# Dealing expert units to three weight streams, and taking a norm's root before its reciprocal

## What is computed

```python
def rmsnorm(x, g):                       # four times in the first block
    return x * rsqrt(mean(x * x) + 1e-6) * g

def layer_norm(x, g, b):                 # four times in the second block
    xc = x - mean(x)
    return xc * rsqrt(mean(xc * xc) + 1e-6) * g + b

def hier_moe(h, ...):                    # once in each of two layers
    # each token takes one of 4 groups and in it the best 2 of 8 experts
    ...
    order = jnp.argsort(flat_e)
    counts = jnp.bincount(flat_e, length=32)
    # the tokens of each expert are padded to whole blocks
    def run(args):
        xb, e = args
        return (jax.nn.silu(xb @ w1[e]) * (xb @ w3[e])) @ w2[e]
    ...
    # each token gets the sum of its two experts' rows, weighted by the gates
```

## Time and profile before

| | us |
|---|---|
| runs (three) | 3443.96, 3446.84, 3448.02; median 3446.84 |
| the profiled execution's own time | 3443.93 |
| its span, first to last instruction | 3442.1 |
| PE busy | 2927.2 (85% of the span) |
| DVE busy | 1152.2 (33%) |
| ACT busy | 681.0 (20%) |
| GpSimd busy | 123.5 (4%) |
| granted TensorE clock, mean | 0.920 of full |
| HBM read, written | 611.4 MB, 37.2 MB |

### The profile page before, as it was taken

The page is one execution under the profiler, slowest core; times in us unless marked ns, Lnnn a source line. Parts: engine busy times, 40 slices in busy tenths (PEclk is TensorE's granted clock), DMA queues, the critical chain, the costliest instruction groups (busy, mean ns, idle before and its releaser), DMA issues. The chain is left out here.

```text
span 3442.1 us, 38147 instructions
## 1 busy us (share of the span) xinstructions
PE 2927.2 (85%) x14080; PEld 1621.7 (47%) x14081; DVE 1152.2 (33%) x2252; ACT 681.0 (20%) x1368; POOL 123.5 (4%) x185
## 2 busy tenths in 40 slices
PE   6979867897999988996885989899688785999995
PEld 3435545544444443555553545444444543554553
DVE  2330178605887312026534111111323723111113
ACT  2430146401000000114422000000121521000002
POOL 0000000000000000000000100000100001000100
PEclk9999979998999998997996999999788897999997
DMA  4222200025755421110014999999712015999993
GB/s 171 81 77 86 108 7 1 0 73 144 299 220 204 174 79 61 61 49 31 0 54 166 389 407 394 403 405 411 273 60 80 0 54 199 396 394 416 375 409 124
DMA packets 137721, 631.50 MB, mean 183 GB/s; under 512 B 19270, under 2 KB 32966, under 8 KB 86560
## 3 DMA queue, kind: packets, MB, share of 16 engines
q1 hardware_dynamic: 93280, 418.20, 31.9%
q10 hardware_dynamic: 34992, 191.12, 13.8%
q0 software_dynamic: 9360, 21.00, 1.7%
HBM read 611.39 MB, written 37.22 MB: 188 GB/s over the span
## 5 line engine op out<-in xcount | busy, mean ns | idle before, releaser
L158 PE MATMUL psum<-normed,weight_ring 128*128 128x512 f32 x1472 | 642.9, 599 | 36.3 <-PEq L192 17.8
L158 PEld LDWEIGHTS psum<-normed,weight_ring 128*128 128x128 f32 x1472 | 282.8, 192 | 393.4 <-issue 393.4
L2106 PE MATMUL psum<-weight_ring,slot_rows_turned 128*64 128x256 f32 x3456 | 397.2, 383 | 1.0 <-issue 1.0
L2106 PEld LDWEIGHTS psum<-weight_ring,slot_rows_turned 128*64 128x64 f32 x3456 | 246.4, 138 | 147.2 <-issue 33.2
L2106 PE MATMUL psum<-third_stream_weights,slot_rows_turned 128*64 128x256 f32 x1728 | 219.6, 412 | 61.9 <-DMA third_stream_weights<-in_w_dram 61.8
L949 DVE SCALAR_TENSOR_TENSOR psum<-weight_ring,condition_rows 128x1024 f32<-128x1024 f32 x192 | 236.9, 1234 | 15.4 <-issue 0.9
L158 PE MATMUL psum<-modulated,weight_ring 128*128 128x384 f32 (+2 forms) x640 | 228.7, 518 | 0.0
L2238 DVE COPY expert_hidden_turned<-psum 128x256 f32<-128x256 f32 x81 | 34.3, 424 | 513.4 <-PE psum L2114 513.4
L2106 PEld LDWEIGHTS psum<-third_stream_weights,slot_rows_turned 128*64 128x64 f32 x1728 | 131.3, 149 | 149.9 <-DMA third_stream_weights<-in_w_dram 70.2
L2121 PE MATMUL psum<-weight_ring,expert_hidden_turned 128*64 128x512 f32 x864 | 197.2, 598 | 0.0
L2229 DVE COPY slot_rows_turned<-psum 128x512 f32<-128x512 f32 x81 | 56.0, 691 | 402.7 <-PE psum L2085 402.7
(11 more groups left out here) (362 smaller groups left out, 3069.4 us busy)
## 6 DMA issues: line engine op xcount, KB each, us to landing
weight_ring<-in_w_dram SPq DMA_DIRECT2D x114, 2048.0 KB, 15.1
third_stream_weights<-in_w_dram ACTq DMA_DIRECT2D x81, 2048.0 KB, 19.1
weight_ring<-in_w_ada_dram SPq DMA_DIRECT2D x24, 2048.0 KB, 9.9
weight_ring<-in_w_ffn_dram SPq DMA_DIRECT2D x11, 2048.0 KB, 7.8
expert_rows<-expert_rows ACTq DMA_DIRECT2D x162, 128.0 KB, 12.6
weight_ring<-in_w_rnn_dram SPq DMA_DIRECT2D x8, 1536.0 KB, 14.1
weight_ring<-in_w_att_dram SPq DMA_DIRECT2D x6, 2048.0 KB, 7.6
weight_ring<-in_w_in_dram SPq DMA_DIRECT2D x6, 2048.0 KB, 9.6
```

The costliest lines, as they stand in the source:

```text
L158: last = nc.tensor.matmul(out, weights[:, k * P:(k + 1) * P], rhs(k), start=(k == 0), stop=(k == tiles - 1))
L2106: last = nc.tensor.matmul(ps[64 * o:64 * o + 64, 2 + b, 256 * m:256 * (m + 1)], XT[:, b, k % 4, 64 * (k // 4):64 * (k // 4) + 64], w[:, k, ...
```

## The change

1. `rms_norms` and `layer_norm`: ACT takes the root of the variance straight from PSUM, with epsilon as the bias (a column `c.eps`, filled once), and DVE takes the reciprocal of the root just before it scales that piece. The additions are gone, and so is the signal from DVE to ACT; ACT waits for PE's variance instead. In `rms_norms` piece 0 is scaled before piece 1 is inverted.
2. `route`: experts other than 0 and 31 with one unit or none are `single`, the others `several`. With `nfirst = n - 2 * nhalf`, the `several` that end past `nfirst` are moved behind all singles, and the singles forward by as many units. Stream 0 takes only units 0 to nfirst-1 (so that it comes short where n is no multiple of three), the third stream the nhalf units from nfirst on, stream 1 the last nhalf as before. The table's third expert and the keys follow `nfirst` in place of `nhalf`.
3. The constants of the router have 32 more columns (`inner`), and the table's columns are 24 in place of 20.

The code of the experts' stage itself is not changed.

```diff
@@ -149,6 +149,7 @@
         c.nc.vector.memset(c.mean_w[:, :], 1.0 / D)
         if c.stat_count == 1:
             c.nc.vector.memset(c.ones[:, :], 1.0)
+            c.nc.vector.memset(c.eps[:, :], EPS)
 yield
 
 
...
@@ -201,8 +202,10 @@
                 finished.wait(act, (s - 1) * npiece + i + 1)
             nc.scalar.activation(sq[:, :, cols(i)], src[:, :, cols(i)], ACT.Square).then_inc(squared.sem, 1)
         for i in range(npiece):
-            inverted.wait(act, s * npiece + i + 1)
-            nc.scalar.activation(c.rstd[:, cols(i)], c.rstd_sq[:, cols(i)], ACT.Sqrt).then_inc(rooted.sem, 1)
+            u = s * npiece + i
+            var_ready.wait(act, u + 1)
+            nc.scalar.activation(c.stat[:, cols(i)], ps[:, u, 0:NORM_WIDTH], ACT.Sqrt, bias=c.eps[:, 0:1])\
+                .then_inc(rooted.sem, 1)
 
 @block.tensor
 def _(pe):
...
@@ -218,15 +221,11 @@
 v = nc.vector
 for s, (src, gain, out, add_to) in enumerate(stages):
     for i in range(npiece):
-        u = s * npiece + i
-        var_ready.wait(dve, u + 1)
-        v.tensor_scalar(c.stat[:, cols(i)], ps[:, u, 0:NORM_WIDTH], EPS, None, ALU.add)
+        rooted.wait(dve, s * npiece + i + 1)
+        v.reciprocal(c.rstd[:, cols(i)], c.stat[:, cols(i)])
+        if first and i == 0:
+            dve.wait_ge(c.consts_landed, 16 * len(c.const_loads))
         dve.drain()
-        v.reciprocal(c.rstd_sq[:, cols(i)], c.stat[:, cols(i)]).then_inc(inverted.sem, 1)
-    if first:
-        dve.wait_ge(c.consts_landed, 16 * len(c.const_loads))
-    for i in range(npiece):
-        rooted.wait(dve, s * npiece + i + 1)
         for k in range(KT):
             last = v.scalar_tensor_tensor(out=out[:, k, cols(i)], in0=src[:, k, cols(i)],
                                           scalar=c.vec(gain, k), in1=c.rstd[:, cols(i)],
...
@@ -1649,16 +1648,12 @@
 if 2 <= step < npiece + 2:
     i = step - 2
     rooted.wait(dve, i + 1)
+    v.reciprocal(VAR[:, 1, cols(i)], VAR[:, 0, cols(i)])
+    dve.drain()
     for k in range(KT):
         x = X[:, k, cols(i)]
-        v.scalar_tensor_tensor(out=x, in0=x, scalar=c.vec(gain, k), in1=ROOT[:, cols(i)],
+        v.scalar_tensor_tensor(out=x, in0=x, scalar=c.vec(gain, k), in1=VAR[:, 1, cols(i)],
                                op0=ALU.mult, op1=ALU.mult).then_inc(scaled.sem, 1)
-if 1 <= step < npiece + 1:
-    i = step - 1
-    var_ready.wait(dve, i + 1)
-    v.tensor_scalar(VAR[:, 0, cols(i)], ps[:, i, 0:WIDTH], EPS, None, ALU.add)
-    dve.drain()
-    v.reciprocal(VAR[:, 1, cols(i)], VAR[:, 0, cols(i)]).then_inc(inverted.sem, 1)
 if modulated and 3 <= step < npiece + 3:
     i = step - 3
     shifted.wait(dve, i + 1)
...
@@ -1683,8 +1678,9 @@
     a.activation(SQ[:, :, cols(step)], X[:, :, cols(step)], ACT.Square).then_inc(squared.sem, 1)
 if 1 <= step < npiece + 1:
     i = step - 1
-    inverted.wait(act, i + 1)
-    a.activation(ROOT[:, cols(i)], VAR[:, 1, cols(i)], ACT.Sqrt).then_inc(rooted.sem, 1)
+    var_ready.wait(act, i + 1)
+    a.activation(VAR[:, 0, cols(i)], ps[:, i, 0:WIDTH], ACT.Sqrt, bias=c.eps[:, 0:1])\
+        .then_inc(rooted.sem, 1)
 if 2 <= step < npiece + 2:
     i = step - 2
     for k in range(KT):
...
@@ -1896,17 +1892,40 @@
 v.tensor_reduce(nunits, units, AX, ALU.add)
 v.tensor_scalar(TS[:, 0, 0:NEXP], units, 1.0, None, ALU.min)
 dve.drain()
+second_from, third_by, turned_by, at = (TC[:, 13 + n:14 + n] for n in (0, 1, 2, 5))
+nfirst, nsingle, nmoved = (TC[:, 20 + n:21 + n] for n in range(3))
+single, several, scratch = TS[:, 3, 0:NEXP], TS[:, 3, NEXP:NKEY], TS[:, 4, 0:NEXP]
 v.tensor_tensor(earlier, by_pair(rank, 1), by_pair(rank, 2), ALU.is_gt)
-dve.drain()
-v.tensor_tensor(earlier, earlier, by_pair(units, 1), ALU.mult)
-dve.drain()
-v.tensor_reduce(base, earlier, AX, ALU.add)
-dve.drain()
-v.tensor_tensor(ends, base, units, ALU.add)
 v.scalar_tensor_tensor(out=TS[:, 1, 0:NEXP], in0=count[:, 1:NEXP + 1], scalar=float(NSTREAM),
                        in1=nunits.broadcast_to([P, NEXP]), op0=ALU.mult, op1=ALU.is_lt, accum_out=nrounds)
 v.tensor_scalar(TC[:, 10:11], nunits, 3.0, 1.0, ALU.mult, ALU.add)
 v.tensor_scalar(TC[:, 17:18], nunits, 3.0, -4.0, ALU.mult, ALU.add)
+v.scalar_tensor_tensor(out=single, in0=units, scalar=1.0, in1=const("inner"), op0=ALU.is_le, op1=ALU.mult)
+dve.drain()
+v.tensor_tensor(earlier, earlier, by_pair(units, 1), ALU.mult)
+v.tensor_scalar(nhalf, nrounds, 1.0, None, ALU.add)
+v.scalar_tensor_tensor(out=scratch, in0=single, scalar=1.0, in1=units, op0=ALU.mult, op1=ALU.mult,
+                       accum_out=nsingle)
+v.tensor_tensor(several, const("inner"), single, ALU.subtract)
+dve.drain()
+v.tensor_reduce(base, earlier, AX, ALU.add)
+v.scalar_tensor_tensor(out=nfirst, in0=nhalf, scalar=-2.0, in1=nunits, op0=ALU.mult, op1=ALU.add)
+v.tensor_tensor(second_from, nunits, nhalf, ALU.subtract)
+dve.drain()
+v.tensor_tensor(ends, base, units, ALU.add)
+v.tensor_scalar(third_by, nfirst, -3.0, 2.0, ALU.mult, ALU.add)
+v.scalar_tensor_tensor(out=turned_by, in0=nfirst, scalar=3.0, in1=TC[:, 17:18], op0=ALU.mult, op1=ALU.add)
+v.tensor_scalar(at, const("number"), nfirst, None, ALU.add)
+dve.drain()
+v.scalar_tensor_tensor(out=several, in0=ends, scalar=nfirst, in1=several, op0=ALU.is_gt, op1=ALU.mult)
+dve.drain()
+v.scalar_tensor_tensor(out=base, in0=several, scalar=nsingle, in1=base, op0=ALU.mult, op1=ALU.add)
+v.scalar_tensor_tensor(out=scratch, in0=several, scalar=-1.0, in1=units, op0=ALU.mult, op1=ALU.mult,
+                       accum_out=nmoved)
+dve.drain()
+v.scalar_tensor_tensor(out=base, in0=single, scalar=nmoved, in1=base, op0=ALU.mult, op1=ALU.add)
+dve.drain()
+v.tensor_tensor(ends, base, units, ALU.add)
 
 oh = OH[:, :, 0:nt, :]
 both = lambda n: V1[:, n, :, 0:nt]
...
@@ -1922,18 +1941,12 @@
 v.tensor_tensor(jb, n4(both(8), NCAPS - 1), row4(caps[:, 1:], NCAPS - 1), ALU.is_ge)
 dve.drain()
 v.tensor_reduce(b, jb, AX, ALU.add)
-v.tensor_scalar(nhalf, nrounds, 1.0, None, ALU.add)
-dve.drain()
-second_from, third_by, turned_by, at = (TC[:, 13 + n:14 + n] for n in (0, 1, 2, 5))
-v.tensor_tensor(second_from, nunits, nhalf, ALU.subtract)
-v.tensor_scalar(third_by, nhalf, -3.0, 2.0, ALU.mult, ALU.add)
-v.scalar_tensor_tensor(out=turned_by, in0=nhalf, scalar=3.0, in1=TC[:, 17:18], op0=ALU.mult, op1=ALU.add)
-v.tensor_scalar(at, const("number"), nhalf, None, ALU.add)
+dve.drain()
 v.tensor_tensor(blk, b, both(9), ALU.add)
 v.scalar_tensor_tensor(out=place, in0=b, scalar=-float(CAP), in1=both(8), op0=ALU.mult, op1=ALU.add)
 dve.drain()
 v.tensor_scalar(both(9), blk, -6.0, turned_by, ALU.mult, ALU.add)
-v.tensor_scalar(both(6), blk, nhalf, third_by, ALU.is_ge, ALU.mult)
+v.tensor_scalar(both(6), blk, nfirst, third_by, ALU.is_ge, ALU.mult)
 dve.drain()
 v.scalar_tensor_tensor(out=both(9), in0=blk, scalar=second_from, in1=both(9), op0=ALU.is_ge, op1=ALU.mult)
 v.scalar_tensor_tensor(out=both(6), in0=blk, scalar=3.0, in1=both(6), op0=ALU.mult, op1=ALU.add)
...
@@ -1957,7 +1970,7 @@
 v.scalar_tensor_tensor(out=TS[:, 4, 0:NEXP], in0=base, scalar=at, in1=count[:, 0:NEXP],
                        op0=ALU.is_le, op1=ALU.mult)
 dve.drain()
-v.scalar_tensor_tensor(out=KEYS[:, 2, 0:NEXP], in0=base, scalar=nhalf, in1=KEYS[:, 1, 0:NEXP],
+v.scalar_tensor_tensor(out=KEYS[:, 2, 0:NEXP], in0=base, scalar=nfirst, in1=KEYS[:, 1, 0:NEXP],
                        op0=ALU.is_lt, op1=ALU.mult)
 v.scalar_tensor_tensor(out=KEYS[:, 2, NEXP:NKEY], in0=ends, scalar=second_from, in1=KEYS[:, 1, NEXP:NKEY],
                        op0=ALU.is_gt, op1=ALU.mult)
...
@@ -2433,6 +2446,7 @@
 consts[:, KAT["desc"]] = NEXP - np_.arange(NEXP)
 consts[:, KAT["order"]] = -np_.arange(NEXP)
 consts[:, KAT["order"]][:, list(FIXED)] = [FAR, -FAR]
+consts[:, KAT["inner"]] = ~np_.isin(np_.arange(NEXP), FIXED)
 consts[:, KAT["caps"]] = CAP * np_.arange(NCAPS)
 consts[:, KAT["iota"]] = np_.arange(P)
 experts_twice = np_.arange(NKEY) % NEXP
```

More of the change, by code:

```diff
@@ L141, in stat_buffers @@
         c.stat_count = c.stat_count + 1
-        c.rstd, c.rstd_sq, c.stat = (ctx.enter_context(c.nc.sbuf_tensor(f"{n}{c.stat_count}", [P, T], F32))
-                                     for n in ("rstd", "rstd_squared", "stat"))
+        c.rstd, c.stat = (ctx.enter_context(c.nc.sbuf_tensor(f"{n}{c.stat_count}", [P, T], F32))
+                          for n in ("rstd", "stat"))
         c.mean_w = ctx.enter_context(c.nc.sbuf_tensor(f"mean_weights{c.stat_count}", [P, P], F32))
@@ L187, in rms_norms @@
     nc, ph, ps = c.nc, c.ph, c.ps
-    squared, inverted, rooted, finished = ph[0:4]
+    squared, rooted, finished = ph[0], ph[2], ph[3]
     var_ready = c.sig("ln_var_ready")
@@ L238, in _ @@
                     last.then_inc(finished.sem, 1)
-    for s in (squared, inverted, rooted, finished, var_ready):
+    for s in (squared, rooted, finished, var_ready):
         s.passed(len(stages) * npiece)
@@ L1059 @@
 KAT = {}
-for _name, _width in (("desc", NEXP), ("order", NEXP), ("caps", NCAPS), ("iota", P), ("movable", NKEY), ("expert", NKEY), ("stream", NKEY),
```

(12 more changed lines are left out.)

## The result

The changed kernel takes 3403.32 us (median of 4 runs, 3399.41 to 3404.92) against 3445.4 us for the kernel before (4 runs, 3438.5 to 3448.02): ratio 0.9879, 95% interval 0.9862 to 0.9896. Forecast: 3413, range 3397 to 3427.

A forecast was written before the change was run, and what follows sets the result against it. Expert rounds run at PE's pace plus 84.6 us of waits for weights. Experts 24.1, norms 7.4 and 5.9, less plan 3.4, make 34.0 us: 3409.9 against the profiled run, 3412.8 against the median, said 3413, range 3397 to 3427.

The forecast's parts named there:

- The list of loads: Expert stages: ring loads fall from 34 to 27, that is from 102 issues to 81.
- The six terms of the forecast: Waits lost in layer 0's rounds 1, 4, 12 and layer 1's 1, 10, 11: 24.1 us in all.
- Round 3's 6.8: Layer 0's round 3 keeps its 6.8 us wait, since load 12 stays and removing load 13 gains 0.
- The queues: DMA engines take turns between queues, so a load behind another in its queue takes nothing from the third stream's.
- Pair after the mixer: The two norms after the mixer end 4.2 us sooner, with piece 0's first scaling 3.3 us sooner.
- Norm after the feed-forward: This single norm gains 1.6 us: 3.3 less the 1.75 reciprocal now between its pieces.
- The two with a router: Layer norms with a router, where PE's products pace the end: about 1.0 and 1.1 us gained.
- Last norm: The last layer norm gains 0.4 us.
- C: Norms: reciprocals stand bare on VectorE, so only the first-scaling gain of 4 us stays; 3422 us, chance 0.11.
- D: Router plan: tokens fall otherwise or other loads are issued, so only norms and plan count; 3437 us, chance 0.06.
- E: PE's clock drops to 1.2 GHz in expert rounds without pauses, making it slower; two such rounds give 3471, chance 0.04.
- B: Expert stages: DMA time is one purse, round 3's wait goes too; expert term 35 to 40, 3397 to 3402, chance 0.14.

The follow-up runs named there:

- e2: The kernel before with only the norms' change (root ahead of the reciprocal), old deal of units: 3428.69 us, ratio 0.9956.
- e7: The kernel before with only ScalarE's order changed in the layer norms, the next piece's root behind the bias pass: 3442.19 us, ratio 0.9998.
- e4: The changed kernel with the third stream's w2 loaded once a layer, its later units using the wrong w2: 3374.43 us.
- e10: The kernel before with the third stream's w1 and w3 issued one unit earlier, nothing else changed: 3427.8 us, ratio 0.9953.
- e1: The kernel before with only the new deal of units (plan and constants), old norms: 3421.94 us, ratio 0.9934.
- e3: The changed kernel with the third stream's w1 and w3 issued one unit earlier: 3383.08 us, ratio 0.9825.
- e6: The changed kernel with stream 0 as long as before: several-unit experts still moved, empty units back on the third stream: 3428.88 us.

## Why the prediction was right, point by point

**The list of loads** held to the issue: 81 for 102, and seven experts of bytes.

In the profiled executions the drop is 40.1 us for the 34.0 of the forecast: 2.3 more in the experts, 1.6 more in the norms, 0.3 less lost in the plans, and 1.9 in code that is the same, which no term held. The time came 9.5 us under the forecast's 3413.

**Rounds.** The six terms of the forecast, 1.7, 8.1, 2.4, 2.2, 7.0 and 2.7, came out as 1.8, 8.1, 2.4, 2.2, 7.0 and 2.7: a round that loses its wait falls to 35.28 and no further. Round 3's 6.8 stayed (7.6). The experts gave 26.4 for 24.1. The missing term is the tail behind round 12 in layer 0, 17.09 us before and 15.45 after, which no window of the forecast held, 1.6; the other 0.7 is the sum of shifts of up to 2.0 us either way in rounds 3 and 6 to 11 of layer 0 and 6 and 7 of layer 1. Such shifts come without the deal too: with the old deal (e2) round 1 of layer 0 took 39.36 us for 37.03 and round 4 41.11 for 43.37. The single rounds' agreement is thus partly luck. The length of layer 0's stage can be trusted to 1 us; layer 1's is less firm with the old deal, 464.1 us before, 467.7 in e2 and 461.1 in e7.

**The queues.** The Trainium skill (DMA: Bandwidth & Descriptors, section Queues, rings and completion order) says that each DMA engine takes turns between queues with work. The traces agree: 24.2 and 24.7 us to landing for round 3's slower chunk, with and without load 13 behind load 12 in the other queue, and 14.1 for round 4's, where that queue was empty when they were issued. In e4 the consequence is seen once more: w2 behind them in their own queue is gone, and round 3's slower chunk still takes 23.3 us and the wait stays.

**The norms** gave 14.9 us for 13.3, with the parts mis-sized and the errors cancelling:
- Pair after the mixer: 1.1 for 4.2. The failed step is that durations were taken as fixed. TensorE's granted clock is 0.62 over the first mean, mostly the lower level of 1.2 GHz, where it was 1.00, the full 2.4, so the stretch of square and mean takes 8.91 us for 6.23. It does not need the new norm: e10 has the old one, shows 0.62 there too, and needs 40.34 us for the pair. But all eight traces with the new norms have it and only one of four with the old, so the change may well bring it on by what it shifts; how isn't shown. Against that trace the new norm's 37.04 is 3.3 us better, near the forecast. The first mean and the whole pair in e10:

```profile
777.75:786.70 8.95, 6.48 (x17) 5.24 (x18) 0.16 (x1) 4.99 (x3) 0.00 (x0) 0.62 0.65 236
```

```profile
777.75:818.09 40.34, 18.91 (x65) 15.00 (x65) 25.94 (x43) 10.52 (x10) 0.00 (x0) 0.73 0.14 52
```

- Norm after the feed-forward: 3.05 for 1.6. Here PE's 32 matmuls take 7.17 us for 8.86, and the first mean is there 1.7 us sooner after its start, so 1.7 us is clock and 1.35 the norm. All eight traces with the new norms have the 7.17, and the four with the old have 8.86 or more, so this gain of clock comes with the change each time; how isn't shown.
- The two with a router: 1.45 and 2.24 for 1.0 and 1.1. In the second PE is busy 1.2 us less for the same 116 matmuls, the likely source of the excess.
- Between the layers: 3.35 for 3.4.
- Last norm: 2.92 for 0.4. The forecast kept ScalarE's passes as what paces all pieces. With two pieces only, the first bias pass, held back behind a root, was all that stood ahead of the last one; e7 gets 2.6 us from the order alone.
- First norm: 0.8 for 1.6, in these two traces. Over all of them, from the first square to the last scaling, the mean is 20.1 us with the old norm (four) and 18.6 with the new (eight), so 1.5.

**The plan** cost 1.3 and 1.8 us for 1.7 each; in e1 1.96 and 1.75.

**Rivals.** C fell by e2, D by the count of issues. E did not come: every clean round has the clock at 1.00. B was wrong where it was tested in the forecast, but e3 and e4 show that bytes do limit rounds 6 to 11 of layer 0 as a whole.

**Left open.** Why the clock falls at the first mean in every trace with the new norms and in one of four with the old; why order alone (e7) gives nothing in the router norms; how the last waits of layer 0 (rounds 6, 8 and 10 in e3) would go. Six rounds at PE's pace are 211.7 us, which at 421 GB/s hold 89 MB, and e3 moved 101 MB in that stretch (241.7 us at 419 GB/s), so by this estimate two experts' loads of 6.29 MB fewer at positions 19 to 34 would have to bring it: not tried. And e3 itself, 3383 us, beats both kernels.

## What to carry to other kernels

Count loads by where they fall, not by their sum: a removed load is worth the wait that stood against it (0 to 8 us here for the same 6.29 MB), and fewer loads can be slower if the rest bunch up (e6). A wait in a round with a low DMA share (0.68 with a wait of 7 us, e4) is one for lead time; a share near 1 says nothing by itself (round 3 waits 6.8 us at 1.01 in the kernel before, and keeps that wait). Cure a wait for lead time by issuing earlier, which here gave 20 us on the changed kernel, about as much as the whole new deal (e1), and 15 on the kernel before. Once the transfers no longer pause, what counts is bytes in that stretch. Where engines work in order, look at what an instruction at the head of the queue holds up, but try the order alone before the gain is put down to it.

## What was not expected of the hardware

- Two hardware queues with 2 MB loads in them carry 419 to 422 GB/s over whole rounds, with a DMA share of 1.01 to 1.02, in every round with a wait in e10 and in layer 0's rounds 6, 8 and 10 of e3, and 419 over six rounds together (e3).
- The granted clock during the first mean after the mixer is either 1.00 or 0.62 over 6 to 9 us, after the same work and a pause of 3.5 us in which PE waits for ScalarE's square. The kernel before and e10 have the same code up to there, and their pairs of norms differ by 2.2 us (38.14 and 40.34). A forecast of that stage to a microsecond can't be had from one trace.
- The kernel before spreads over 3435.6 to 3454.5 us in all its runs, e3 over 2.6 us in four; the parts of a few us were told apart by stage lengths in single traces and not by medians.
